# First mixer of a two-block transformer kernel: the gates and both output projections are computed with tokens on the partitions

## What is computed

```
u = rmsnorm(x, norm_mix_g) @ w_in            # 1024 -> 5376 columns
u_rwkv, u_attn, u_gate = split(u, [1792, 3328])
o_a = rwkv7_time_mix(u_rwkv, ...)            # 256 x 512
o_b = diff_attention(u_attn, ...)            # 256 x 512
g_a, g_b = split(sigmoid(u_gate), 2)         # 256 x 1024 each
merged = g_a * (o_a @ w_proj_a) + g_b * (o_b @ w_proj_b)
x = x + merged @ w_out
h = rmsnorm(x, norm_mlp_g)                   # and on to the MLP
```

## Time and profile before

| what | value |
|---|---|
| the three runs | 1449.74, 1448.24, 1449.86 us (median 1449.74) |
| span of the profiled execution | 1447.7 us |
| instructions in it | 22866 |
| TensorE, weight load | 1434.0 us (99%), 1233.0 us (85%) |
| VectorE, ScalarE, GpSimd | 1013.2 us (70%), 769.4 us (53%), 29.4 us (2%) |
| HBM | 246.59 MB read, 171 GB/s over the span |

### The profile page before, as it was taken

How to read it: one execution, slowest core, us unless ns; L and a number is a source line. 1 busy time by engine, 2 the same in 40 slices (tenths; PEclk the granted TensorE clock), 3 DMA queues, 4 the chain that set the end, 5 groups by cost and what they waited for, 6 DMA issues and landing times.

```text
span 1447.7 us, 22866 instructions
## 1 busy us (share of the span) xinstructions
PE 1434.0 (99%) x9408; PEld 1233.0 (85%) x9408; DVE 1013.2 (70%) x1341; ACT 769.4 (53%) x1047; POOL 29.4 (2%) x96
## 2 busy tenths in 40 slices
PE   9999999999999999999999999999999999999999
PEld 8988898888887888888878888888888887788887
DVE  6876567886356787548768877478774688687753
ACT  7744564654336565445665554355553556665542
POOL 0000000000001200000000000000000000000000
PEclk9999999999999999999999999999999999999999
DMA  8431235555544455544424555545555453255552
GB/s 337 169 119 63 87 117 204 198 202 203 190 159 175 156 220 179 202 174 180 170 88 157 193 199 182 201 158 205 190 189 191 152 196 123 94 207 188 190 188 87
DMA packets 36104, 249.11 MB, mean 172 GB/s; under 512 B 4129, under 2 KB 4257, under 8 KB 6689
## 3 DMA queue, kind: packets, MB, share of 16 engines
q1 hardware_dynamic: 35712, 247.46, 47.2%
q10 hardware_dynamic: 288, 0.19, 0.0%
HBM read 246.59 MB, written 1.05 MB: 171 GB/s over the span
## 4 chain that ended last, share of the span: by engine, by line
PE 66%; DVE 1%; issue 0%; POOL 0%; ACT 0%; DVEq 0%; ACTq 0%; POOLq 0%
PE ps L1995 20%; PE ps L2002 10%; PE ps L1910 10%; PE ps L1912 10%; PE ps L1911 10%; PE ps L1985 2%; PE ps L1984 1%; PE ps L2328 1%; PE ps L2308 1%; PE ps L2052 1%; PE ps L2317 0%; PE ps L2256 0%; DVE lo L2685 0%; PE ps L1981 0%; PE ps L2290 0%
## 5 line engine op out<-in xcount | busy, mean ns | idle before, releaser
L2685 DVE TENSOR_TENSOR lo<-raw,hi 128x2048 fp32r<-128x2048 f32 (+1 forms) x230 | 525.3, 2285 | 226.7 <-ACT hi L2359 226.5
L2359 ACT CAST hi<-raw 128x2048 fp32r<-128x2048 f32 (+1 forms) x230 | 438.0, 1905 | 249.0 <-PE ps L1912 245.2
L1995 PE MATMUL ps<-h,hi 128*128 128x512 f32 x1472 | 351.5, 390 | 0.0
L1995 PEld LDWEIGHTS ps<-h,hi 128*128 128x128 f32 x1472 | 270.5, 188 | 51.3
L1910 PE MATMUL ps<-hi,a 128*128 128x512 f32 x584 | 230.2, 394 | 0.0
L1912 PE MATMUL ps<-hi,a 128*128 128x512 f32 x584 | 227.6, 390 | 0.0
L1911 PE MATMUL ps<-lo,a 128*128 128x512 f32 x584 | 227.3, 389 | 0.0
L2002 PEld LDWEIGHTS ps<-h,lo 128*128 128x128 f32 x1472 | 188.1, 190 | 7.7
L2002 PE MATMUL ps<-h,lo 128*128 128x256 f32 x1472 | 190.3, 282 | 0.0
L2548 ACT COPY a<-ps 128x256 f32<-128x256 f32 x208 | 76.3, 372 | 203.7 <-PE ps L1995 100.9
L1910 PEld LDWEIGHTS ps<-hi,a 128*128 128x128 f32 x584 | 109.6, 188 | 24.1 <-issue 2.0
(11 more groups left out here) (347 smaller groups left out, 1595.9 us busy)
## 6 DMA issues: line engine op xcount, KB each, us to landing
raw<-ws SPq DMA_DIRECT2D x229, 1024.0 KB, 4.8
X<-xin SPq DMA_DIRECT2D x8, 256.0 KB, 5.3
raw<-ws SPq DMA_DIRECT2D x2, 512.0 KB, 6.3
out<-X SPq DMA_DIRECT2D x4, 256.0 KB, 2.1
small<-small SPq DMA_DIRECT2D x1, 992.5 KB, 12.6
const<-const SPq DMA_DIRECT2D x1, 900.0 KB, 6.6
a<-row SPq DMA_DIRECT2D x1, 512.0 KB, 7.0
const<-const SPq DMA_DIRECT2D x1, 388.0 KB, 13.1
```

The costliest lines, as they stand in the source:

```text
L1995: t = e.matmul(b2(s["slots"][u]), wh[:, k, 128 * u:128 * u + 128], h2[:, k, :, :], start=k == 0, stop=last)
L2359: e.copy(hi[j % NSPL][:, n], raw[j % NRAW][:, n]).then_inc(hi_ready, 1)
L2685: e.tensor_tensor(lo[j % NSPL][:, n], raw[j % NRAW][:, n], hi[j % NSPL][:, n].bitcast(F), ALU.subtract).then_inc(lo_ready, 1)
```

## The change

The eight pieces of the gates and the four pieces of the two projections are laid out 512 columns wide and computed in the rows form. The gates are now scaled by the token's factor as a scalar of each partition. The products with the gates and the sum are made with tokens on the partitions. `w_out` needs the sum with its columns on the partitions, so TensorE transposes it: four groups of four transposes (`m_turn`), one for each half of the columns and half of the tokens. ACT copies a turned bank to `mH`, and DVE takes `mL` from the same bank. The turn of (half 0, b 0) stands between the two pieces of `w_proj_a`, that of (0, 1) after four steps of the second piece, that of (1, 0) ahead of `w_out`, and that of (1, 1) after the first four steps of `w_out`. x is loaded again after the last turn.

```diff
@@ stream_plan
-    cols("w_in", 0, 8, 3328, 2048, 256)
+    for c in range(3328, 5376, 512):
+        deep("w_in", 0, 8, c, 512)
@@ buffers
-        gB = Arena(0)([128, 8, S])
+        gB = Arena(0)([128, 2, D])
-        gA = X[:, :, :].rearrange("p b (n s) -> p (b n) s", s=S)
+        gA = X
@@ mixers_fill (ga and gb fall away)
+            def gate_in(g, half):
+                def evac(sl, b, h):
+                    emit("gate_in", dve=0.7, slot=sl, g=g, b=b, half=half, rstd=nm.rstd)
+                    state["g" + g, half] = sl
+                return evac
+
+            for g, c in (("A", 3328), ("B", 4352)):
+                for half in range(2):
+                    yield from rows_mat("w_in", 0, 8, c + 512 * half, 512, "h", nm.h_needs, gate_in(g, half))
             yield "pe"
             while "ob" not in state or "gates" not in state:
                 yield None
-                yield from cols_piece("w_proj_b", 0, c, "ob", lambda k: (diff_v.sem, state["ob_v"]), pb)
+                yield from rows_mat("w_proj_b", 0, 4, 512 * half, 512, "ob", lambda k, b: (diff_v.sem, state["ob_v"]),
+                                    pb(half))
@@ behind the weave
-        for c in range(0, 1024, 512):
-            straight(cols_piece("w_proj_a", 0, c, "oa", ..., pa))
-        emit("x_again", v=merge_v.n)
+        def m_turn(half, b):
+            sl = take()
+            emit("m_turn", slot=sl, b=b, half=half, v=merged[half, b], v_hi=merge_a.add())
+            give(sl)
+            m_at[half, b] = (free[sl.b], sl.n)
+        straight(rows_mat("w_proj_a", 0, 4, 0, 512, "oa", oa_needs, pa(0)))
+        m_turn(0, 0)
+        spread(rows_mat("w_proj_a", 0, 4, 512, 512, "oa", oa_needs, pa(1)), [lambda: m_turn(0, 1)], 4)
+        m_turn(1, 0)
-        straight(rows_into_x("w_out", 0, 8, "m", lambda k, b: (merge_v.sem, 2 * (k // 2) + 2), x_add((1.0, 1.0)), nm))
+        def last_turn():
+            m_turn(1, 1)
+            emit("x_again", last=m_at[1, 1])
+        spread(rows_into_x("w_out", 0, 8, "m", lambda k, b: m_at[k // 4, b], x_add((1.0, 1.0)), nm), [last_turn], 4)
@@ tensor_program
+                elif kind == "m_turn":
+                    claim(sl)
+                    e.wait_ge(merge_v.sem, s["v"])
+                    for u in range(4):
+                        c = 512 * s["half"] + 128 * u
+                        t = e.transpose(banks[sl.b][:, 128 * u:128 * u + 128], gA[:, s["b"], c:c + 128], ident)
+                    t.then_inc(full[sl.b], 1)
@@ scalar_program
-                    e.copy(mH[:, n:n + 2, :], gA[:, n:n + 2, :]).then_inc(merge_a.sem, 1)
+                    ready(sl)
+                    e.copy(mH[:, k:k + 4, 128 * b:128 * b + 128], b4(sl)).then_inc(merge_a.sem, 1)
@@ vector_program
+                elif kind == "gate_in":
+                    b, o = s["b"], slice(512 * s["half"], 512 * s["half"] + 512)
+                    e.wait_ge(rstd_ready.sem, s["rstd"])
                     ready(sl)
+                    e.tensor_scalar({"A": gA, "B": gB}[s["g"]][:, b, o], banks[sl.b][:, :], rstd[b], None,
+                                    ALU.mult).then_inc(free[sl.b], 1)
@@ pa: the same product and sum, on [:, b, o]; then
+                elif kind == "m_turn":
                     e.wait_ge(merge_a.sem, s["v_hi"])
-                    e.tensor_tensor(mL[:, n:n + 2, :], g, mH[:, n:n + 2, :].bitcast(F), ALU.subtract).then_inc(merge_v.sem, 1)
+                    e.tensor_tensor(mL[:, k:k + 4, out_], b4(sl), mH[:, k:k + 4, out_].bitcast(F),
+                                    ALU.subtract).then_inc(free[sl.b], 1)
```

More of the change, by code:

```diff
@@ L1554, in mixers_fill, with pb, evac @@
                 yield None
[L1556 to L1559, removed]
-            for c in range(0, 1024, 512):
-                if c:
+            def pb(half):
+                def evac(sl, b, h):
+                    emit("pb", dve=0.7, slot=sl, b=b, half=half, sig=state["sig", "B", half])
+                return evac
+            for half in range(2):
+                if half:
                     yield "pe"
@@ L1571, in program, with pa, evac, oa_needs @@
               [mixers_fill(nm)])
[L1573 to L1580, removed]
-        emit("x_again", v=merge_v.n)
+        m_at = {}
+        merged = {}
+        def pa(half):
+            def evac(sl, b, h):
+                emit("pa", slot=sl, b=b, half=half, sig=state["sig", "A", half], v=merge_v.add())
+                merged[half, b] = merge_v.n
+            return evac
+        def m_turn(half, b):
[3 more added lines that the diff above has]
+            m_at[half, b] = (free[sl.b], sl.n)
+        def oa_needs(k, b):
+            return (rwkv_v.sem, max(rwkv_v.at["oal0"], rwkv_v.at["oal1"]))
+        straight(rows_mat("w_proj_a", 0, 4, 0, 512, "oa", oa_needs, pa(0)))
+        m_turn(0, 0)
+        spread(rows_mat("w_proj_a", 0, 4, 512, 512, "oa", oa_needs, pa(1)), [lambda: m_turn(0, 1)], 4)
+        m_turn(1, 0)
         for b in range(2):
@@ L2532, in scalar_program @@
                 elif kind == "gate_sig":
-                    part = {"A": gA, "B": gB}[s["g"]][:, 4 * s["half"]:4 * s["half"] + 4, :]
+                    part = {"A": gA, "B": gB}[s["g"]][:, :, 512 * s["half"]:512 * s["half"] + 512]
                     if s["table"]:
@@ L2537, in scalar_program @@
                     e.activation(part, part, ACT.Sigmoid).then_inc(gate_a.sem, 1)
-                elif kind == "pa":
-                    n = s["n"]
-                    e.wait_ge(merge_v.sem, s["v"])
-                    e.copy(mH[:, n:n + 2, :], gA[:, n:n + 2, :]).then_inc(merge_a.sem, 1)
+                elif kind == "m_turn":
+                    b, k = s["b"], 4 * s["half"]
+                    ready(sl)
+                    e.copy(mH[:, k:k + 4, 128 * b:128 * b + 128], b4(sl)).then_inc(merge_a.sem, 1)
                 elif kind == "half":
@@ L2982, in vector_program @@
                 elif kind == "pb":
-                    n = s["n"]
+                    b, o = s["b"], slice(512 * s["half"], 512 * s["half"] + 512)
                     e.wait_ge(gate_a.sem, s["sig"])
                     ready(sl)
-                    e.tensor_tensor(gB[:, n:n + 2, :], b2(sl), gB[:, n:n + 2, :], ALU.mult).then_inc(free[sl.b], 1)
+                    e.tensor_tensor(gB[:, b, o], banks[sl.b][:, :], gB[:, b, o], ALU.mult).then_inc(free[sl.b], 1)
                     read_out(sl)
@@ L2988, in vector_program @@
                 elif kind == "pa":
-                    n = s["n"]
-                    g = gA[:, n:n + 2, :]
+                    b, o = s["b"], slice(512 * s["half"], 512 * s["half"] + 512)
                     e.wait_ge(gate_a.sem, s["sig"])
                     ready(sl)
-                    e.tensor_tensor(g, b2(sl), g, ALU.mult).then_inc(free[sl.b], 1)
+                    e.tensor_tensor(gA[:, b, o], banks[sl.b][:, :], gA[:, b, o], ALU.mult).then_inc(free[sl.b], 1)
                     read_out(sl)
-                    e.tensor_tensor(g, g, gB[:, n:n + 2, :], ALU.add).then_inc(merge_v.sem, 1)
+                    e.tensor_tensor(gA[:, b, o], gA[:, b, o], gB[:, b, o], ALU.add).then_inc(merge_v.sem, 1)
+                elif kind == "m_turn":
+                    b, k = s["b"], 4 * s["half"]
+                    out_ = slice(128 * b, 128 * b + 128)
@@ L3253, in sync_program @@
                 elif kind == "x_again":
-                    e.wait_ge(merge_v.sem, s["v"])
+                    e.wait_ge(s["last"][0], s["last"][1])
                     for b in range(2):
```

21 lines of the change are left out of this document (removed).

## The result

The kernel after takes **1458.28 us** in the median of four runs (1457.16 to 1460.50), the kernel before 1449.80 us beside it. The ratio is 1.0063, with an interval of 1.0049 to 1.0078: some 8.5 us slower, where 1.2 were forecast and 1454.0 us was the upper end of the range.

A forecast was written before the change was run, and what follows sets the result against it. TensorE, 99% busy, was taken to bound the kernel. -1.55 - 0.8 + 1.8 + 1.4 + 0.4 = +1.2 us on the 1447.7 us span gives 1448.9; with 2.0 us between span and median, 1450.9 us; range 1447.0 to 1454.0.

The forecast's parts named there:

- The weave: Recurrence's track ahead of `w_proj_a`: 15.8 us of TensorE work cover 14.5, so no wait; bounds 0 and 3.6 us.
- My own sign of being wrong: Prediction is wrong if the stretch from 104 us to the start of `w_out` shrinks or grows by over 3 us.
- Rival C: First matmul of `w_proj_a`: recurrence runs out of cover, TensorE waits up to 3.6 us more, 1454.5 us; chance 0.18.
- Gates: Eight gate pieces inside the weave: rows form takes 5.554 us a piece for 5.746, 1.55 us saved.
- rival D: Gates in the weave: a rows step costs twice a cols step, 0.239 us, saving gone, 1452.5 us; chance 0.08.
- Projections: Four pieces of the two projections: 5.45 us each in rows form for 5.65, 0.8 us saved.
- Turns: Four groups of transposes on TensorE around `w_proj_a` and `w_out`: 0.45 us each, 1.8 us added.
- Waits at the turns: TensorE waits for VectorE's sums: about 1.4 us at turn (0, 0), another 0.4 at turn (1, 0).
- rival A: At the turns: one `lo` split moves ahead of the last `pb`, both waits vanish, 1449.1 us; chance 0.22.
- x again: Loads of x after the last remainder: the first sum with x comes 3 us later, so cost nothing.
- Rival B: In the weave: hidden waits of 0.9 us go at two or three places, about 1446.5 us, faster; chance 0.10.
- the repacking: Gates, projections and transposes together, without waits: 1.55 + 0.8 - 1.8 = 0.6 us saved.

The follow-up runs named there:

- e1: The kernel after the change, with the planner counting 0.72 us instead of 0.681 for a rows step of the gates: 1449.80 us, ratio 1.0004.
- e6: Against the kernel before, only the gates in rows form (projections in cols form, no turns), planner's count 0.72 us: 1446.61 us, ratio 0.9989.
- e3: The kernel after the change, but with the gates in their old cols form; both projections and the turns as changed: 1451.19 us, ratio 1.0019.
- e5_kept_warm: The kernel after the change, with unread identity matmuls filling both TensorE gaps (14 and 20 of them): 1456.45 us, ratio 1.0054.
- e10_held_until_head2_turned: The kernel after the change, count 0.681, turns placed later, last four gate pieces begun only behind head 2's turn: 1454.13 us, ratio 1.0037.

## Why the prediction was wrong

**The step that failed is "The weave".** I took the recurrence's track, with 14.5 us of latency against 15.8 of cover, and concluded that no wait was to be taken. The track that broke was another: differential attention's head 3, needed two pieces earlier, by the first matmul of `w_proj_b`. From `d_turn` to that matmul it is 211.79 - 201.34 = 10.45 us, over which the script had 3.2 us of work. I had even named the lever, "the planner, whose own costs favour rows steps (0.681 for 0.72)", and then assumed that it would keep the places. The runs showed +7.26 us of gaps and +1.6 us of clock in place of 0, outside my bounds of 0 to 3.6. My own sign of being wrong was met: the start of `w_out` moved from 228.25 to 237.71 us, by more than 3.

**Rival C** had the right kind of mechanism, cover that runs out, at the wrong place (the first matmul of `w_proj_a`, for o_a) and too cheap (3.6 us): I priced the cover's loss by the shorter fill and not by a reordering of the script, and left out the clock. TensorE has no idle time at `w_proj_a` in the change, nor in e1, where no gap ahead gives the recurrence more time.

**Gates, forecast -1.55.** From a marker at 93 us (the same instruction in each trace) to the first matmul of `w_proj_b` it is 112.36 us before and 110.63 in e1: -1.73. e6 says -1.9 by the medians. Right, and rival D falls.

**Projections, forecast -0.8.** The steps of the projections behind the weave are 0.2333 us and not the 0.2272 of `w_out`. Four pieces save 4 x (48 x 0.1178 - 24 x 0.2333) = 0.2 us. The price was taken from a neighbour that doesn't hold for them; why the two stretches differ no run here shows. A pair of narrow matmuls costs here 2 x 117.8 - 233.3 = 2.3 ns more than a wide one, and in the gates 1.73 us / 192 = 9.0 ns. The Trainium skill, page "TensorE: Matmul & The Clock Gate", section "Back-to-back issue gap", has 2.5 ns for each isolated matmul: the projections agree with it, the gates don't, and which of the two a stretch will show no run here settles.

**Turns, forecast +1.8.** 0.44 us each, measured on the fourth. Right.

**Waits at the turns, forecast +1.4 and +0.4.** With the gates in their old form 1.39 and 0.18 us (e3). In the change and in e1 0.44 and some 0.2, since one split had moved ahead of the last `pb`. That is the condition of **rival A**, and still the waits didn't vanish as it says: VectorE stood 1.28 us (1.18 in e1) for ScalarE's rounding in place of the split, a step that neither the forecast nor the rival had. The mechanism was right. The split moved at either count (0.681 and 0.72), so its place goes with the gates' form and not with the number. That e3 came out near 2.8 us is in part luck: it saved 0.2 and not 0.8 us, and waited 0.18 and not 0.4; its trace has 254.85 - 205.91 = 48.94 us from `w_proj_b` to `w_ff1`, +3.1 against before.

**x again, forecast 0.** The loads were asked for at 242.84 us and the first sum that needs them, at 253.60, has no idle time. Right.

**The sum, redone** for the change, up to the first matmul of `w_ff1`: -1.73 + 7.26 + 1.58 for the clock, and then -0.2 + 4 x 0.44 + 0.44 + 0.21 = 2.2 for projections, turns and waits, is +9.3 us. The traces show, from the marker, (261.40 - 93.61) - (251.49 - 93.27) = +9.57 us. The 0.3 us between the two are mostly in the gaps: idle times are printed from modelled ends, and where 7.26 us are printed the filler of e5_kept_warm takes 3.12 + 4.38 = 7.50.

With 0.34 us from ahead of the marker the change is 9.91 us late at `w_ff1`, and yet the span grew by 8.1 only: 1.8 us came back later, 1.5 of them at one place. At one and the same step of the next block (a group of four transposes that waits for `nt`) TensorE stands for 1.85 us before, at 482.04, and for 1.84 us after, at 491.96. Before, its clock fell behind that. Windows of before:

```profile
480.00:484.00 4.00, 2.15 (x11) 1.81 (x11) 1.84 (x5) 2.52 (x4) 1.19 (x6) 0.84 0.73 236
484.00:488.00 4.00, 4.00 (x19) 3.44 (x19) 3.90 (x5) 0.90 (x2) 0.00 (x0) 0.73 0.36 119
```

and of after:

```profile
488.00:492.00 4.00, 2.16 (x13) 1.63 (x12) 2.55 (x3) 4.00 (x6) 3.06 (x6) 1.00 0.21 51
492.00:496.00 4.00, 4.00 (x24) 3.55 (x25) 3.28 (x4) 0.82 (x2) 0.00 (x0) 1.00 0.52 215
```

The other traces settle that this isn't the change's doing. At this step, behind an idle time of 1.77 to 1.86 us, the clock falls to 0.50 for some 3 us in four of the thirteen (before, e1, e5, e6) and stays at 1.00 in the nine others, with early and late heads among both. The runs agree: of the 57 later ones of the kernel before, the 41 with a mean clock of 1.000 took 1447.76 to 1449.10 us and the 16 with 0.999 took 1449.19 to 1450.35. The four in the result above hold three above 1449.7. Against the median of 1448.55 us of 21 runs the change is 9.7 us slower, which is about the 9.6 of the traces. What decides in one execution whether the clock falls there stays open.

The reading for e1, where the order is good and the clock falls at that step as it does before, is -1.73 + 2.16 (48.02 - 45.86 from `w_proj_b` to `w_ff1`) = +0.4 us, with a measured ratio of 1.0004, where the forecast was +1.2. The 0.8 us between them are the waits at the turns (0.65 and not 1.8) and the gates (-1.73 and not -1.55), less the projections (-0.2 and not -0.8): errors of 1.2 and 0.6 us that partly cancel. Rival B's "-0.8 to -1.4" should by the same terms begin at the -0.6 of the repacking; it changes nothing in the outcome.

## What to carry to other kernels

Where a planner orders the work, its cost for a step is an input of the kernel like any other: changing the form of a product changes that number, and a change of some 5% in it (0.72 to 0.68) cost 9 us with no matmul changed. Before forecasting such a change, list for every track the last thing that it delivers, who waits for it, and how much fill stands behind it; take the track with the least and not the longest one. And leave the planner's costs as they were when the form changes, so that one thing changes at a time, and try the number by itself afterwards. The number nearest to the trace isn't for that the best one: a rows step of the gates measures some 3 x 0.23 = 0.69 us, and 0.69 is slow here where 0.72 and 0.80 are not.

## What was unexpected of the hardware

- A gap in TensorE's work costs more than its length. TensorE stood for 3.04 us, worked for 0.67 and stood again for 4.22; within that second gap the granted clock fell from 1.00 to 0.50, and the first eight matmuls behind it, of 512 columns, took 3.45 instead of 1.87 us. Identity matmuls in the gaps kept the clock at 1.00 and gave 1.5 us back.
- Gaps of about the same length (1.85 us) at the same step were followed by a lower clock in four of thirteen traces (0.73 from 484 to 488 us, before) and not in the others (1.00 from 492 to 496 us, after). By the mean clocks of its runs it happens in some executions of one kernel and not in others; it cost 1.5 us in the trace of before, about the spread of 1.6 us between the three runs of that kernel. Within one trace, e10_held_until_head2_turned, the clock fell to 0.50 behind an idle time of 1.47 us (158.81) and stayed at 1.00 behind one of 1.48 us (211.68).
- The step of a matmul of 512 columns isn't one number: 0.227 to 0.230 us in the gates (stretches of ten steps and more, in the change and in e1), 0.227 in `w_out`, 0.233 in the projections between them, all at a granted clock of 1.00.
